# Last projection of a two-block transformer kernel: 12 of its 44 2x2 units by seven block products in place of eight

## The chip, the cores and the metric

The kernel runs on one core of one Trainium2 chip, in one launch. The metric is the time of one execution in device microseconds. Before the change it is 2310.49 us, the median of three runs (2310.07 to 2310.59).

## The reference, cut to what matters

The reference is two transformer blocks for 272 and then 256 tokens of 2048 features, in float32. The change touches the last matrix product of the second block and the norm and the residual sum behind it:

```
def conv_ffn(h, w_up, conv_w, w_down):
    ...
    gate, val = jnp.split(c, 2, axis=-1)
    return (jax.nn.silu(gate) * val) @ w_down          # (256, 5632) @ (5632, 2048)

def rms_norm(x, g):
    xf = x.astype(jnp.float32)
    y = xf * lax.rsqrt(jnp.mean(xf * xf, axis=-1, keepdims=True) + RMS_EPS)
    return (y * g.astype(jnp.float32)).astype(x.dtype)
...
    x = x + rms_norm(conv_ffn(h, ffn_w_up[i], ffn_conv[i], ffn_w_down[i]), norm_g[i, 3])
```

## The kernel before

Every large product is done in the type float32r with operands split in two: a high half (the value copied into float32r) and a low half (the value less its high half). A product of two blocks is three matmuls: high by high, high by low and low by high.

Weights come as chunks of 256 rows by 512 columns (512 KB): `raw[:, slot]` holds a chunk as two blocks of 128 rows, `kk` 0 and 1. A ring of four slots (`RING`) carries all 744 chunks of the kernel. Per chunk, four engines work in this order. SyncE's queue loads it (`raw`) when the low half of the chunk four earlier is done (`low_ready`). ScalarE copies it to the high half `wh` (function `high`, L584) when it has landed and TensorE has used the chunk four earlier (`chunk_used`). VectorE writes the low half `wl` (function `low`, L1046) when the high half is there. TensorE uses it when the low half is there. Each engine takes its instructions strictly in the order of its own program, so an instruction that waits holds up all behind it.

The last projection is `down2`: 88 chunks, four groups `g` of 512 output columns, 22 chunks `c` each. The activations stay put: `acth` and `actl` hold high and low halves of 44 blocks of 128 features by 256 tokens. TensorE goes through the groups one after the other, and for each chunk through its two row blocks and the two halves of the tokens `t` (L2571 to L2573): twelve matmuls of 128x128 by 128x512 per chunk. Output (`g`, `t`) has its own PSUM bank, `2 * g + t`. In the last group the last four chunks go through `t` = 0 first (`half_done`) and then `t` = 1, so that the first half of the tokens is done earlier.

When a group is through, ScalarE squares its two banks with a sum along the row (`square_rows`, L1010) and VectorE multiplies them by the gain into `ft` (`gain_rows`, L1801). Behind the last group the sum of squares becomes the scale of the row (`spread`: root on ScalarE, reciprocal on VectorE), and VectorE writes scale times `ft` plus the residual `ht` in pieces of 1024 or 512 columns (L1825), which SyncE stores. `ht` is the residual stream turned from feature rows to token rows by 32 transposes of VectorE (`block_of_h`, L1832), one after each of 16 low halves in the second and in the third group. GpSimd has nothing to do in this projection.

Of the kernel before, what the change touches and what calls it, by code (L numbers as in the profile page):

```python
# [21 lines left out]
F32 = mybir.dt.float32  # L22
F32R = mybir.dt.float32r
# [3 lines left out]
P = 128  # L27
# [83 lines left out]

N_PAIRS = 16
# [36 lines left out]
def program(nc, d):  # L149
    with ExitStack() as ctx:  # L150
# [21 lines left out]
        vec = persistent("vec", [P, N_VEC])  # L172
        ident = persistent("ident", [P, P])
# [100 lines left out]
        spent = at("spent", [P, 512], F32, LENT)  # L274

# [47 lines left out]
        ft_ready, out_ready = sem("ft_ready"), sem("out_ready")  # L323

# [186 lines left out]
        def _(pool):  # L511
# [11 lines left out]
            for s, (name, n) in enumerate(SUMS):  # L523
# [31 lines left out]
                for c, m in enumerate(CHUNK_LENGTHS):  # L555
# [13 lines left out]
                    pool.wait_ge(bk_ready, 2 * c + 2)  # L569


        @block.scalar
        def _(act):
# [433 lines left out]
            def square_rows(g, t):  # L1007
                if g + t:
                    act.wait_ge(squared, 2 * g + t)
                act.activation(spent[:], ps[:, 2 * g + t, :], ACT.Square, accum_out=squares[:, t, g:g + 1]).then_inc(squared, 1)  # L1010

            def squares_of_rows(g):
                if g < 3:
                    act.wait_ge(chunk_used, FIRST["down2"] + (g + 1) * CHUNKS["down2"])
                    square_rows(g, 0)
                    square_rows(g, 1)
                    if g == 2:
                        act.activation(warmed[:, 5:6], eps[:], ACT.Sqrt)
                    return
                act.wait_ge(partial_ready, 1)  # L1020
                for t in range(2):
                    if t == 0:
                        act.wait_ge(half_done, 1)
                    else:
                        act.wait_ge(chunk_used, N_CHUNKS)
                    square_rows(g, t)
                    act.wait_ge(squared, 7 + t)
                    act.activation(spread[:, t:t + 1], squares[:, t, 3:4], ACT.Sqrt, scale=1.0 / D,
                                   bias=partial[:, t:t + 1]).then_inc(spread_root, 1)

            plain("down2", squares_of_rows, ahead=8)


        @block.vector
        def _(dve):
# [762 lines left out]
            def gain_rows(g, t):  # L1798
                part = slice(512 * g, 512 * g + 512)
                dve.wait_ge(squared, 2 * g + t + 1)  # L1800
                dve.tensor_tensor(ft[:, t, part], ps[:, 2 * g + t, :], gain[:, part], ALU.mult).then_inc(ft_ready, 1)  # L1801

            def gained_rows(g):
                if g < 3:
                    group_full("down2", g)
                    if g == 0:
                        dve.wait_ge(gain_landed, 16)
                    gain_rows(g, 0)
                    gain_rows(g, 1)
                    if g == 2:  # L1810
                        dve.wait_ge(squared, 6)
                        dve.tensor_reduce(partial[:], squares[:, :, 0:3], mybir.AxisListType.X, ALU.add).then_inc(dve_step, 1)
                        dve.wait_ge(dve_step, steps.add())
                        dve.tensor_scalar(partial[:], partial[:], 1.0 / D, RMS_EPS, ALU.mult, ALU.add).then_inc(partial_ready, 1)
                    return
                dve.wait_ge(ht_ready, 32)
                for t in range(2):
                    gain_rows(g, t)
                    dve.wait_ge(spread_root, t + 1)
                    dve.reciprocal(spread[:, t:t + 1], spread[:, t:t + 1]).then_inc(spread_ready, 1)  # L1820
                    dve.wait_ge(spread_ready, t + 1)
                    dve.wait_ge(ft_ready, 7 + t)
                    for row, f0, f1 in OUT_PARTS:
                        if row == t:
                            dve.scalar_tensor_tensor(ft[:, t, f0:f1], ft[:, t, f0:f1], spread[:, t:t + 1], ht[:, t, f0:f1],  # L1825
                                                     ALU.mult, ALU.add).then_inc(out_ready, 1)

# [7 lines left out]
            def rows_of_h(g):  # L1835
                first, per = FIRST["down2"], CHUNKS["down2"]
                start = first + g * per + RING
                lows(start, 1, start % RING)
                gained_rows(g - 1)
                if g == 1:  # L1840
                    dve.wait_ge(h_ready, 48)
                for x in range(1, per):
                    low(start + x, (start + x) % RING)
                    if 2 <= x < 18:
                        block_of_h(16 * (g - 1) + x - 2)

# [11 lines left out]
        def _(pe):  # L1858
# [827 lines left out]
```

## Time and profile before

| | us |
|---|---|
| median of three runs | 2310.49 |
| the profiled execution, from start to end | 2310.11 |
| its span in the profile | 2308.0 |
| TensorE busy | 2297.3 |
| VectorE busy | 1558.6 |
| ScalarE busy | 1071.4 |
| GpSimd busy | 111.7 |
| the last projection's matmuls, first start to last start | 245.17 |

In the profile PE is TensorE's matmul, PEld its weight load, DVE is VectorE, ACT is ScalarE, POOL is GpSimd, SP is SyncE. A row of a group has the line of the program, the engine, the operation, the tile that is written and those that are read, the shape, the count, and behind the bar the busy time in all and the mean of one in ns, then the idle time of the engine just ahead of these instructions and what ended it. The granted clock of TensorE is 0.999 of full speed over the span. PE's busy time counts each matmul until it has drained, so consecutive matmuls overlap: their rate is read from the starts.

### The profile page before, as it was taken

Reading aid. Unit: us, or ns where it says so; the run is one execution under the profiler, and the core shown is the slowest. Engines: PE = TensorE matmul, PEld = TensorE weight load, DVE = VectorE, ACT = ScalarE, POOL = GpSimd, SP = SyncE. Lnnn points to the kernel's source line nnn. Section 1 sums busy time; section 2 is a strip of 40 time slices with the busy share of each in tenths; the row PEclk is TensorE's granted clock in tenths of the full one; section 3 lists DMA queues with packets and bytes.
Section 4 is the critical chain, followed back from the end, with each engine's and each line's share of the span. In section 5 each row is a group of like instructions: output and inputs, shape, how many; then the busy total and the mean of one; then the engine's idle time right before and its main releaser. Section 6 shows DMA issues by size and latency. Waiting matters only on the chain.

```text
span 2308.0 us, 49207 instructions
## 1 busy us (share of the span) xinstructions
PE 2297.3 (100%) x19330; PEld 2097.1 (91%) x19330; DVE 1558.6 (68%) x2008; ACT 1071.4 (46%) x1365; POOL 111.7 (5%) x144
## 2 busy tenths in 40 slices
PE   9999999999999999999999999999999999999998
PEld 9999999999999999998889999899888888888887
DVE  5688877748766666665444867559877777784664
ACT  6543444455444444444444556655444444444343
POOL 2000000012000000000000200012000000000000
PEclk9999999999999999999999999999999999999999
DMA  7554334355665665666556574465565665656664
GB/s 256 178 160 132 110 103 134 133 189 175 190 188 182 185 185 186 182 190 184 191 185 186 154 245 130 126 196 161 183 191 192 184 195 174 200 178 215 190 186 151
DMA packets 115688, 406.92 MB, mean 176 GB/s; under 512 B 12864, under 2 KB 17824, under 8 KB 115168
## 3 DMA queue, kind: packets, MB, share of 16 engines
q1 hardware_dynamic: 110672, 396.03, 55.1%
q10 hardware_dynamic: 4880, 8.87, 1.1%
q8 instruction: 111, 1.82, 0.3%
q14 instruction: 25, 0.20, 0.0%
HBM read 402.70 MB, written 2.15 MB: 175 GB/s over the span
## 4 chain that ended last, share of the span: by engine, by line
PE 98%; DVE 1%; ACT 0%; issue 0%; DVEq 0%; POOL 0%; ACTq 0%; POOLq 0%
PE ps L1919 26%; PE ps L1921 13%; PE ps L1924 8%; PE ps L1925 8%; PE ps L1926 8%; PE ps L2573 4%; PE ps L2571 4%; PE ps L2572 4%; PE ps L2131 3%; PE ps L2121 2%; PE ps L2123 2%; PE ps L2122 2%; PE ps L1884 2%; PE ps L1883 2%; PE ps L1882 2%; PE ps L2487 1%
## 5 line engine op out<-in xcount | busy, mean ns | idle before, releaser
L1046 DVE TENSOR_TENSOR wl<-raw,wh 128x1024 fp32r<-128x1024 f32 x742 | 906.9, 1234 | 623.8 <-ACT wh L584 622.2
L584 ACT ACTIVATE wh<-raw 128x1024 fp32r<-128x1024 f32 x742 | 776.6, 1057 | 898.6 <-PE ps L1921 370.1
L1919 PE MATMUL ps<-x,wh 128*128 128x512 f32 x1280 | 448.0, 393 | 0.0
L1924 PE MATMUL ps<-xx,wh 128*128 128x258 f32 (+3 forms) x1320 | 375.0, 284 | 0.0
L1925 PE MATMUL ps<-xx,wh 128*128 128x258 f32 (+3 forms) x1320 | 373.6, 283 | 0.0
L1926 PE MATMUL ps<-xx,wl 128*128 128x258 f32 (+3 forms) x1320 | 373.2, 283 | 0.0
L1921 PE MATMUL ps<-x,wl 128*128 128x256 f32 x1280 | 357.1, 279 | 0.0
L1919 PEld LDWEIGHTS ps<-x,wh 128*128 128x128 f32 x1280 | 239.8, 187 | 57.1
L1924 PEld LDWEIGHTS ps<-xx,wh 128*128 128x128 f32 x1320 | 248.2, 188 | 2.1 <-issue 0.8
L1925 PEld LDWEIGHTS ps<-xx,wh 128*128 128x128 f32 x1320 | 248.3, 188 | 0.4
L1926 PEld LDWEIGHTS ps<-xx,wl 128*128 128x128 f32 x1320 | 248.3, 188 | 0.0
L1921 PEld LDWEIGHTS ps<-x,wl 128*128 128x128 f32 x1280 | 239.8, 187 | 0.0
L1919 PE MATMUL ps<-xx,wh 128*128 128x512 f32 x640 | 225.0, 395 | 0.0
L1919 PE MATMUL ps<-act,wh 128*128 128x512 f32 x528 | 185.4, 393 | 0.0
L1921 PE MATMUL ps<-xx,wl 128*128 128x256 f32 x640 | 179.9, 281 | 0.0
L1921 PE MATMUL ps<-act,wl 128*128 128x256 f32 x528 | 149.3, 283 | 0.0
L1919 PEld LDWEIGHTS ps<-xx,wh 128*128 128x128 f32 x640 | 120.3, 188 | 27.9
L2573 PE MATMUL ps<-wh,act 128*128 128x512 f32 x352 | 138.9, 395 | 0.0
L2571 PE MATMUL ps<-wh,act 128*128 128x512 f32 x352 | 138.9, 395 | 0.0
L2572 PE MATMUL ps<-wl,act 128*128 128x512 f32 x352 | 138.9, 395 | 0.0
L1921 PEld LDWEIGHTS ps<-xx,wl 128*128 128x128 f32 x640 | 120.5, 188 | 0.0
L1919 PEld LDWEIGHTS ps<-act,wh 128*128 128x128 f32 x528 | 99.2, 188 | 22.9
(361 smaller groups left out, 3876.6 us busy)
## 6 DMA issues: line engine op xcount, KB each, us to landing
raw<-in_gate_up SPq DMA_DIRECT2D x176, 512.0 KB, 3.7
raw<-in_down SPq DMA_DIRECT2D x176, 512.0 KB, 4.2
raw<-in_up SPq DMA_DIRECT2D x176, 512.0 KB, 3.7
raw<-in_w_in SPq DMA_DIRECT2D x103, 512.0 KB, 3.8
raw<-in_in SPq DMA_DIRECT2D x48, 512.0 KB, 4.2
raw<-in_w_out SPq DMA_DIRECT2D x32, 512.0 KB, 4.4
raw<-in_out SPq DMA_DIRECT2D x32, 512.0 KB, 3.7
bias<-bias_rows ACTq DMA_DIRECT2D x1, 4096.0 KB, 25.9
```

The source lines that it names most:

```text
L584: act.activation(wh[:, slot], raw[:, slot], ACT.Copy).then_inc(high_ready, 1)
L1046: dve.tensor_tensor(wl[:, slot], raw[:, slot], wh[:, slot].bitcast(F32), ALU.subtract).then_inc(low_ready, 1)
L1882: pe.matmul(out, w_high, hi, start=(k == 0), stop=False)
L1919: pe.matmul(ps[:, 4 * parity + m, :].rearrange("p (s n) -> p s n", s=2), w_high, hi, start=(k == 0), stop=False)
L1921: last = pe.matmul(out, w_low, hi[:, 0], start=False, stop=(k == 2 * per - 1))
L1924: pe.matmul(out, w_high, high, start=(k == 0), stop=False)
L1925: pe.matmul(out, w_high, low, start=False, stop=False)
L1926: last = pe.matmul(out, w_low, high, start=False, stop=(k == 2 * per - 1))
L2131: last = pe.matmul(ps[o:o + rows, b, C * f:C * f + n], lhs[HEAD_ROWS[e]], rhs[HEAD_ROWS[e]], start=start, stop=stop)
L2571: pe.matmul(out, acth[:, k, tokens], wh[:, slot, kk, :], start=(k == 0), stop=False)
L2572: pe.matmul(out, acth[:, k, tokens], wl[:, slot, kk, :], start=False, stop=False)
L2573: last = pe.matmul(out, actl[:, k, tokens], wh[:, slot, kk, :], start=False, stop=(k == 2 * per - 1))
```

## The change

The output columns are now taken in two halves `p` of two column blocks `x` each, and the chunks are reordered on the host so that the chunks of a row pair `c` for both column blocks follow each other. Two such chunks are a unit: two row blocks by two column blocks of weights, against two token halves by two row blocks of activations, eight block products. 32 of the 44 units are done that way. In 12 (`SEVEN`) the 2x2 product is done by seven products (Winograd's form of Strassen's scheme), with sums of blocks on both sides: four mixed blocks of activations, four mixed blocks of weights. Four of the seven products are gathered in the four PSUM banks of the other half; behind the last seven-unit of a half, ScalarE copies the first of them to `ft` and VectorE adds up the corrections there (`combine`), and when the half is through adds each bank to its corner (`add_corner`).

GpSimd makes the four mixed activation blocks (from the sum of high and low halves) and, after ScalarE's high half, their low half. VectorE makes the mixed weights `mixes` from `raw`, ScalarE their high halves and VectorE their low halves. Only three of the four weight blocks of a seven-unit need halves of their own. The transposes now come two per eight-unit in the first half and one in the second. The squares are taken from `ft` and not from PSUM. The last two row pairs of the second half are done corner by corner.

The core of the diff:

```
+SEVEN = [(7, 10, 13, 16, 19), (3, 6, 8, 11, 13, 16, 18)]
+CORNERS = [(0, 0), (1, 0), (0, 1), (1, 1)]
...
 # GpSimd
+            for p in range(2):
+                for c in SEVEN[p]:
+                    q = SEVENTH[p][c]
+                    if q:
+                        pool.wait_ge(act_mix_ready, q)
...
+                    step(pool.tensor_tensor(whole_act[:], acth[:, 2 * c:2 * c + 2, :].bitcast(F32),
+                                            actl[:, 2 * c:2 * c + 2, :].bitcast(F32), ALU.add))
...
+                    pool.tensor_tensor(act_mix[:, 3], a11, a21, ALU.subtract)
+                    step(pool.tensor_tensor(act_mix[:, 0], a21, a22, ALU.add))
+                    step(pool.tensor_tensor(act_mix[:, 1], act_mix[:, 0], a11, ALU.subtract))
+                    pool.tensor_tensor(act_mix[:, 2], a12, act_mix[:, 1], ALU.subtract).then_inc(act_mixed, 1)
+                    pool.wait_ge(act_mixed, q + 1)
+                    pool.wait_ge(act_mix_split, q + 1)
+                    pool.tensor_tensor(act_mix_low[:], act_mix, act_mix_high[:].bitcast(F32),
+                                       ALU.subtract).then_inc(act_mix_ready, 1)
 # ScalarE
+            def seven_highs(p, c):
...
+                high(n, slot)
+                act.wait_ge(landed[slot + 1], 16 * ((n + 1) // RING + 1))
+                act.wait_ge(chunk_used, n + 1 - (RING - 1))
+                act.activation(wh[:, slot + 1, 1], raw[:, slot + 1, 1], ACT.Copy).then_inc(high_ready, 1)
+                act.wait_ge(act_mixed, q + 1)
+                if q:
+                    act.wait_ge(mix_used, q)
+                act.activation(act_mix_high[:], act_mix, ACT.Copy).then_inc(act_mix_split, 1)
+                for x in range(2):
+                    act.wait_ge(mixed, 2 * q + x + 1)
+                    act.activation(mix_high[x][:], mixes[x], ACT.Copy).then_inc(mix_split, 1)
 # VectorE
+            def mix_weights(p, c):
...
+                dve.wait_ge(landed[slot], 16 * (n // RING + 1))
+                dve.wait_ge(landed[slot + 1], 16 * (n // RING + 1))
+                if q:
+                    dve.wait_ge(mix_split, 2 * q)
+                    dve.wait_ge(mix_ready, 2 * q)
+                dve.tensor_tensor(mixes[0], raw[:, slot + 1], raw[:, slot:slot + 2, 0], ALU.subtract).then_inc(mixed, 1)
+                dve.wait_ge(mixed, 2 * q + 1)
+                step(dve.tensor_tensor(mixes[1][:, 0], raw[:, slot + 1, 1], mixes[0][:, 0], ALU.subtract))
+                dve.tensor_tensor(mixes[1][:, 1], raw[:, slot, 1], mixes[1][:, 0], ALU.subtract).then_inc(mixed, 1)
...
+            def seven_lows(p, c):
...
+                mix_weights(p, c)
+                low(n, slot)
...
+                dve.tensor_tensor(wl[:, slot + 1, 1], raw[:, slot + 1, 1], wh[:, slot + 1, 1].bitcast(F32),
+                                  ALU.subtract).then_inc(low_ready, 1)
+                for x in range(2):
+                    dve.wait_ge(mix_split, 2 * q + x + 1)
+                    dve.tensor_tensor(mix_low[x][:], mixes[x], mix_high[x][:].bitcast(F32), ALU.subtract).then_inc(mix_ready, 1)
...
+            def combine(p):
...
+                dve.wait_ge(first_kept, p + 1)
...
+                step(dve.tensor_tensor(corner(p, 1, 0), ps[:, bank + 2, :], corner(p, 0, 0), ALU.add))
+                step(dve.tensor_tensor(corner(p, 0, 1), ps[:, bank + 3, :], corner(p, 1, 0), ALU.add))
+                dve.tensor_tensor(corner(p, 1, 1), ps[:, bank + 1, :], corner(p, 0, 1), ALU.add)
+                dve.tensor_tensor(corner(p, 1, 0), ps[:, bank + 1, :], corner(p, 1, 0), ALU.add).then_inc(combined, 1)
 # TensorE
+                pe.wait_ge(low_ready, n + 1)
+                product(extra[0], act_of(k, 0), weight_of(slot, 0), start, stop)
+                product(sums[0], act_of(k + 1, 0), weight_of(slot, 1), False, False).then_inc(chunk_used, 1)
+                pe.wait_ge(low_ready, n + 2)
+                pe.wait_ge(act_mix_ready, q + 1)
+                product(sums[2], mixed_act(2), weight_of(slot + 1, 1), False, False).then_inc(chunk_used, 1)
+                pe.wait_ge(mix_ready, 2 * q + 1)
+                product(extra[1], mixed_act(0), mixed_weight(0, 0), start, stop)
+                product(extra[3], mixed_act(3), mixed_weight(0, 1), start, stop)
+                pe.wait_ge(mix_ready, 2 * q + 2)
+                product(extra[2], mixed_act(1), mixed_weight(1, 0), start, stop)
+                product(sums[1], act_of(k + 1, 1), mixed_weight(1, 1), False, False).then_inc(mix_used, 1)
```

`product` is the three matmuls. Where the instructions stand now, at three places. First VectorE in the middle of the projection; before, around the seam of the second and third group (`wl<-raw,wh` is a low half, `ht<-lead` a transpose, `ft<-ps,gain` a gain):

```order
L1046 TENSOR_TENSOR wl<-raw,wh 128x1024
L1832 STREAM_TRANSPOSE ht<-lead 32x16x32
L1046 TENSOR_TENSOR wl<-raw,wh 128x1024 x5
L1801 TENSOR_TENSOR ft<-ps,gain 128x512 x2
L1046 TENSOR_TENSOR wl<-raw,wh 128x1024 x2
```

After, from the first seven-unit (unit 7 of the first half) to the start of the second (`ft<-raw` and `ft<-raw,ft` are the mixed weights, `mix_low<-ft,mix_high` their low halves):

```order
L1892 TENSOR_TENSOR ft<-raw 128x1024
L1894 TENSOR_TENSOR ft<-raw,ft 128x512
L1895 TENSOR_TENSOR ft<-raw,ft 128x512
L1121 TENSOR_TENSOR wl<-raw,wh 128x1024
L1904 TENSOR_TENSOR wl<-raw,wh 128x512
L1908 TENSOR_TENSOR mix_low<-ft,mix_high 128x1024 x2
L1121 TENSOR_TENSOR wl<-raw,wh 128x1024 x2
L1877 STREAM_TRANSPOSE ht<-lead 32x16x32 x2
```

A seven-unit puts three mixing passes ahead of its low halves and two low halves of mixed weights behind them; the transposes stand in pairs behind the eight-units. Second GpSimd, which had no instruction here, has these for each seven-unit (`vec` holds the mixed activations; shapes are partitions by elements):

```order
L608 TENSOR_TENSOR whole_act<-act 128x512
L612 TENSOR_TENSOR vec<-whole_act 128x128
L613 TENSOR_TENSOR vec<-whole_act 128x128
L614 TENSOR_TENSOR vec<-vec,whole_act 128x128
L615 TENSOR_TENSOR vec<-whole_act,vec 128x128
L618 TENSOR_TENSOR act_mix_low<-vec,act_mix_high 128x512
```

The first five of the next unit follow directly on the sixth of this one. Third VectorE at the end of the projection (`sums` is the scale of a row). Before:

```order
L1801 TENSOR_TENSOR ft<-ps,gain 128x512
L1820 RECIPROCAL sums<-sums 128x1
L1825 SCALAR_TENSOR_TENSOR ft<-ft,sums,ht 128x1024 x2
L1801 TENSOR_TENSOR ft<-ps,gain 128x512
L1820 RECIPROCAL sums<-sums 128x1
L1825 SCALAR_TENSOR_TENSOR ft<-ft,sums,ht 128x1024
L1825 SCALAR_TENSOR_TENSOR ft<-ft,sums,ht 128x512 x2
```

After (`ft<-ps,ft` is the add of a bank to its corner):

```order
L1951 RECIPROCAL sums<-sums 128x1
L1946 SCALAR_TENSOR_TENSOR ft<-ft,sums,ht 128x1024
L1929 TENSOR_TENSOR ft<-ps,ft 128x512
L1946 SCALAR_TENSOR_TENSOR ft<-ft,sums,ht 128x1024
L1937 TENSOR_TENSOR ft<-ft,gain 128x512
L1941 TENSOR_REDUCE sums<-squares 128x1
L1942 TENSOR_SCALAR sums<-sums 128x1
L1929 TENSOR_TENSOR ft<-ps,ft 128x512
L1937 TENSOR_TENSOR ft<-ft,gain 128x512
L1951 RECIPROCAL sums<-sums 128x1
L1946 SCALAR_TENSOR_TENSOR ft<-ft,sums,ht 128x1024
L1946 SCALAR_TENSOR_TENSOR ft<-ft,sums,ht 128x512 x2
```

The add of the last corner now stands behind the second row pass of the first token half, a gain and two small sums.

## Rows read from the trace of the kernel before

**Rows 1.** The page: busy time by engine, the chain's shares by engine, and one costly group.

```profile
PE 2297.3 (100%) x19330; PEld 2097.1 (91%) x19330; DVE 1558.6 (68%) x2008; ACT 1071.4 (46%) x1365; POOL 111.7 (5%) x144
...
PE 98%; DVE 1%; ACT 0%; issue 0%; DVEq 0%; POOL 0%; ACTq 0%; POOLq 0%
...
L1046 DVE TENSOR_TENSOR wl<-raw,wh 128x1024 fp32r<-128x1024 f32 x742 | 906.9, 1234 | 623.8 <-ACT wh L584 622.2
```

**Rows 2.** Groups by line, 2050 us on: operation, shapes, count, busy us, mean ns, idle.

```profile
L2573 PE MATMUL ps<-wh,act 128*128 128x512 f32 x352 | 138.9, 395 | 0.0
...
L1046 DVE TENSOR_TENSOR wl<-raw,wh 128x1024 fp32r<-128x1024 f32 x89 | 108.8, 1225 | 99.4 <-ACT wh L584 99.4
L584 ACT ACTIVATE wh<-raw 128x1024 fp32r<-128x1024 f32 x88 | 93.1, 1060 | 137.8 <-PE ps L2573 134.6 <-PE ps L1921 3.2
...
L1832 DVE STREAM_TRANSPOSE ht<-lead 32x512 f32<-32x512 f32 x32 | 22.5, 702 | 0.9
...
L1801 DVE TENSOR_TENSOR ft<-ps,gain 128x512 f32<-128x512 f32 x8 | 5.2, 684 | 6.2 <-ACT spent L1010 6.2
L1825 DVE SCALAR_TENSOR_TENSOR ft<-ft,sums,ht 128x1024 f32<-128x1024 f32 (+1 forms) x5 | 5.1, 1068 | 0.1
L1010 ACT ACTIVATE spent<-ps 128x512 f32<-128x512 f32 x8 | 4.7, 593 | 9.1 <-PE ps L2573 9.0
```

**Rows 3.** Timeline, TensorE, first and last matmul of the last projection: start us, duration us.

```profile
2055.17 0.39 PE L2571 MATMUL ps<-wh,act 128*128 128x512 f32 x1
...
2300.34 0.40 PE L2573 MATMUL ps<-wh,act 128*128 128x512 f32 x1
```

**Rows 4.** Chain that ended last, from the last matmul on: start us, us, what.

```profile
2300.77 0.70 ACT spent L1010 x2
...
2301.49 0.69 DVE ft L1801
...
2302.29 1.28 DVE ft L1825
2303.57 0.66 DVEq L150
2304.23 0.66 DVE ft L1825
```

**Rows 5.** Waits, 2080 to 2300 us: who waited for whom, us in total, times, longest.

```profile
DVE wl L1046 <- ACT wh L584: 93.3, 77, 1.9
```

**Rows 6.** Groups by form, GpSimd, whole run.

```profile
L565 POOL TENSOR_TENSOR bk<-b,pinv 128x128 f32<-128x128 f32 x1 | 0.5, 467 | 0.1
```

**Rows 7.** Groups by form, VectorE, whole run: a split of half a chunk.

```profile
L1041 DVE TENSOR_TENSOR wl<-raw,wh 128x512 fp32r<-128x512 f32 x4 | 2.8, 691 | 0.4 <-ACT wh L647 0.4
```

**Rows 8.** Timeline, VectorE (three rows), then GpSimd (two), 217.5 to 220.5 us.

```profile
217.69 0.69 DVE L1245 TENSOR_TENSOR fac<-kn,pe 128x512 f32<-128x512 f32 x1
218.29 1.77 DVE L1246 TENSOR_TENSOR fac<-z,pe 128x512 f32<-128x512 f32 x1
219.99 1.68 DVE L1374 TENSOR_TENSOR am<-ga,lmask 128x512 f32<-128x512 f32 x1
...
217.73 1.79 POOL L565 TENSOR_TENSOR bk<-b,pinv 128x512 f32<-128x512 f32 x1 [48.61 <-DVE b L1233]
219.60 1.52 POOL L567 TENSOR_TENSOR bk<-z,pinv 128x512 f32<-128x512 f32 x1
```

**Rows 9.** Timeline, VectorE (two rows), then GpSimd (two), 311 to 314.5 us.

```profile
311.26 1.76 DVE L1046 TENSOR_TENSOR wl<-raw,wh 128x1024 fp32r<-128x1024 f32 x1 [1.48 <-ACT wh L584]
313.58 0.69 DVE L1468 TENSOR_TENSOR tn<-tn,ps 128x512 f32<-128x512 f32 x1 [0.57 <-PE ps L2131]
...
310.65 1.29 POOL L565 TENSOR_TENSOR bk<-b,pinv 128x512 f32<-128x512 f32 x1 [49.95 <-PE ps L2131]
312.02 2.05 POOL L567 TENSOR_TENSOR bk<-z,pinv 128x512 f32<-128x512 f32 x1
```

**Rows 10.** DMA issues, 2095 to 2255 us: count, KB each, median us from issue to landing.

```profile
raw<-in_down SPq DMA_DIRECT2D x57, 512.0 KB, 4.3
```

More of the change, by code:

```diff
@@ L109 @@
     _n += _k
+SEVEN = [(7, 10, 13, 16, 19), (3, 6, 8, 11, 13, 16, 18)]
+SEVENTH = [{c: q + sum(map(len, SEVEN[:p])) for q, c in enumerate(rows)} for p, rows in enumerate(SEVEN)]
+SEVENS = [len(SEVEN[0]), len(SEVEN[0]) + len(SEVEN[1])]
+CORNERS = [(0, 0), (1, 0), (0, 1), (1, 1)]
 N_PAIRS = 16
@@ L1796, in _ @@
             feed_forward("up2", True)
[L1798 to L1826, printed above, removed]
             def block_of_h(x):
@@ new lines, in add_corner @@
+            def add_corner(p, e):
+                x, t = CORNERS[e]
+                dve.wait_ge(combined, p + 1)
+                if p and t == 0:
+                    dve.wait_ge(half_done, x + 1)
+                elif p and x == 0:
+                    dve.wait_ge(chunk_used, N_CHUNKS - 2)
+                else:
+                    dve.wait_ge(chunk_used, FIRST["down2"] + 44 * (p + 1))
+                dve.tensor_tensor(corner(p, x, t), ps[:, 4 * p + 2 * x + t, :], corner(p, x, t), ALU.add).then_inc(corner_ready, 1)
@@ new lines, in finish_rows, with spread_of_rows @@
+            def finish_rows(t, x0, x1):
+                for row, f0, f1 in OUT_PARTS[x0:x1]:
+                    dve.scalar_tensor_tensor(ft[:, t, f0:f1], ft[:, t, f0:f1], spread[:, t:t + 1], ht[:, t, f0:f1],
+                                             ALU.mult, ALU.add).then_inc(out_ready, 1)
+            def spread_of_rows(t):
+                dve.wait_ge(spread_root, t + 1)
+                dve.reciprocal(spread[:, t:t + 1], spread[:, t:t + 1]).then_inc(spread_ready, 1)
+                dve.wait_ge(spread_ready, t + 1)
@@ new lines, in _ @@
+            dve.wait_ge(chunk_used, FIRST["down2"])
+            dve.wait_ge(h_ready, 48)
+            blocks = 0
+            for p in range(2):
+                for c in range(6 * (1 - p), 22):
+                    if c in SEVEN[p]:
+                        seven_lows(p, c)
+                    else:
+                        lows(row_chunk(p, c), 2, row_chunk(p, c) % RING)
+                        if p and c in (1, 2):
+                            gain_corner(0, 2 * c - 2)
+                            gain_corner(0, 2 * c - 1)
+                        ahead = min(32, blocks + (1 if p and c < 20 else 2))
+                        for x in range(blocks, ahead):
+                            block_of_h(x)
+                        blocks = ahead
+                    if c == SEVEN[p][-1] + 2:
+                        combine(p)
+                    if p and c == 0:
+                        for e in range(4):
+                            add_corner(0, e)
@@ L2575, in _ @@
                         last.then_inc(chunk_used, 1)
[L2576 to L2577 removed]
+                if t == 0:
+                    last.then_inc(half_done, 1)
 def _features(v):
```

219 lines of the change are left out of this document (155 added, 64 removed).

## The prediction

> **What bounds the kernel now.** I read the page first. Its busy times have TensorE at 2297.3 of 2308.0 us and the chain of waits gives it 98% [rows 1]; the reader sees an engine that is never waited out, so only fewer matmuls, or a new wait of TensorE, can move the time. Then the groups of instructions from 2050 us to the end, which is the last projection: three matmul lines with 352 matmuls each (one of them in [rows 2]) and, beside them, the split of the weights, L584 on ScalarE and L1046 on VectorE. Then the first and the last matmul of that projection in the order of time [rows 3]: 2300.34 - 2055.17 = 245.17 us for 1055 steps, 0.2324 us a matmul. The 395 ns of [rows 2] is one matmul from start to drained; the step is what counts. VectorE's waits there, 93.3 us for ScalarE [rows 5], are slack that the change may use. Last the chain behind the last matmul [rows 4].
>
> I call a unit two row blocks by two column blocks: two loaded chunks, eight products of three matmuls, 24 x 0.2324 = 5.58 us. A seven-unit is 21 x 0.2324 = 4.88 us.
>
> **What is removed.** 12 units lose three matmuls: 36 x 0.2324 = 8.37 us, all on the path. Nothing else leaves it: the chunks that are loaded, 88, and the matmul's shape stay.
>
> **VectorE in a seven-unit.** Durations: 1.23 us for 128x1024 and 0.70 for a transpose [rows 2], 0.69 for 128x512 [rows 7]. Queued behind each other, the next starts 0.09 early (0.69 at 217.69, next at 218.29 [rows 8]), so 1.14 and 0.60. Before, a unit asks for two splits, 2.28. A seven-unit asks for four passes of 1024 columns (first mixed block, whole low half, two mixed low halves) and three of 512: 4 x 1.14 + 3 x 0.60 = 6.36, and 0.12 for each of two waits on its own result: 6.6 us, against 4.88 on TensorE. An eight-unit asks for 2.28 and, with the transposes spread over the units, 0.70 (second half) or 1.40 (first). At the closest spacing, seven then eight, that is 6.6 + 2.98 = 9.6 against 4.88 + 5.58 = 10.46. Alone, VectorE would hold the pace and the extra waits of TensorE inside the unit would be met. ScalarE needs 3 x 1.06 + 2 x 0.6 = 4.4 us in a seven-unit [rows 2] and is not the limit either.
>
> **GpSimd beside it.** GpSimd gets two passes of 128x512 (1.29 us each, the first of its rows in [rows 9]) and four of 128x128 (0.47 [rows 6]) per seven-unit. [Rows 8] shows what such a pass does to VectorE. L1245 takes 0.69; the next, L1246, equally large, takes 1.77 while a GpSimd pass reads; then GpSimd's pass is the one that is long; then VectorE's L1374 takes 1.68. They take turns, whole instruction by whole instruction, and VectorE loses 1.0 to 1.1 us to a pass of 1.2 to 1.3, the pass less some 0.2. In [rows 9] a split of 1.23 takes 1.76 in the same way, but L1468, with one input in PSUM, takes 0.69 in the middle of a GpSimd pass. So the price is 2 x 1.04 + 4 x 0.25 = 3.1 us of VectorE per seven-unit, wherever VectorE has passes with two SBUF inputs queued; transposes, and sums with PSUM, are free of it. The 0.25 is an estimate, 0.47 less 0.2.
>
> The Trainium skill, SBUF — State Buffer, section "Who interferes with whom", has this as a rule: a VectorE instruction with two SBUF inputs and a GpSimd instruction that reads SBUF hold one shared read path in turn, each for its whole length. The traces here agree (0.69 against 1.77 us). One could also argue from averages: over the whole run the split averages 1234 ns, in the last projection, where GpSimd is idle, 1225 [rows 1, 2], 9 ns apart. By that the price would be nothing and the sum would be rival A's; by the turns it is 3.1 us. I take the turns: the average holds few splits that met GpSimd.
>
> **Does it fit then?** Seven then eight in the second half: 6.6 + 3.1 + 2.98 = 12.7 against 10.46, 2.2 us short. This spacing stands at units 6, 11 and 16 of the second half (the seven-units are 3, 6, 8, 11, 13, 16, 18): 6.6 us. Seven, eight, eight there: 15.7 against 16.04, 0.4 to spare, three times after the first, 1.2. In the first half (7, 10, 13, 16, 19) seven, eight, eight: 6.6 + 3.1 + 2 x 3.68 = 17.1 against 16.04, but of that 2.8 is transposes, beside which GpSimd can run: 0 to 1.0 short each. A lead could pay for this: a chunk's high half may be made when TensorE has used the chunk four earlier, and by the walk above (high, then low, behind two mixing passes) the low half of a seven-unit is done some 3.5 us before TensorE asks. That pays for the first half, 0 to 5 short. It doesn't pay in the second, because the lead goes round a ring: a chunk is loaded only when the low half four chunks earlier is done, takes 4.3 us to land [rows 10], and the mixing waits for both landed chunks of the unit. 4.3 + 2.6 for the mixes + 2.1 for the two long GpSimd passes + 1.7 for the low halves is 10.7 per two units, against 10.46. So 6.6 - 1.2 = 5.4 in the second half and about nothing in the first; with a rest of lead I take 5.0 us of TensorE waits. The ends are 0 (GpSimd's passes fall into gaps and beside transposes) and 9.6 (6.6 with no recovery, and 3 of the first half).
>
> **The seam between the halves.** TensorE's wait for the combined sums is met if VectorE gets to them in time. Their four passes (0.68 each, one input in PSUM, 2.7 us) stand behind the splits of the first half's last unit, whose inputs are there while TensorE does unit 20, with over a unit left: nothing, or a microsecond or two if VectorE comes late; that is in the range. The gains and sums of the four corners (8 x 0.68 = 5.4 us) fall among five units without sevens, with 5 x (5.58 - 2.98) = 13 us to spare.
>
> **The tail.** Now the last matmul (ends 2300.57 as a step) is followed by the square at 2300.77, the gain, the reciprocal and three row passes ending 2304.89, and then the store [rows 4]: 4.3 us plus the store. After, an add of 0.68 comes ahead of the square, and VectorE is not free. With E the end of matmuls and 2.79 us for each of the four last corners, the second corner's sum is there at E - 5.4. VectorE's queue from there: add to -4.7, wait for the square (0.70) to -3.9, gain to -3.1, reciprocal and a row pass of 1.28 to -1.7, third add to -1.1, the other row pass to +0.1, gain to +0.8, the two small sums to +1.0, and only then the last add, to +1.7. The square starts at +1.75 in place of +0.2: 1.6 us later, 0.7 for the add and 0.8 of queue. From there the chain is the old one.
>
> **Sum.** -8.4 + 5.0 + 1.6 = -1.8 us. The profiled execution took 2310.11 us (span 2308.0 and 2.1 around it), 0.4 under the median of 2310.49. 2310.1 - 1.8 = 2308.3 us. A measurement can tell 0.2%, 4.6 us, from no change; so this is no change.
>
> **Rival A: GpSimd costs VectorE nothing.** -8.4 + 1.6 = -6.8: 2303.3 us, 0.29% faster. For it: VectorE waits 93.3 us in this stretch, there are free slots for 12 x 4.4 us of GpSimd. Against it: the sums and low halves of the activations follow directly on ScalarE's split of the same unit, when VectorE has its longest queue. It holds if the waits stay under 2.2 us. 0.30.
>
> **Rival B: VectorE becomes the bound in every stretch.** If each long GpSimd pass costs VectorE 1.7 us, as L565 and L567 took when they were themselves held up (1.79, 2.05 [rows 8, 9]), the price is 4.4 us a seven-unit, 1.3 more. The pairs are then 3.5 short, 10.5; the triples of the second half 0.9, 2.7; those of the first up to 2.3, 5 to 9, less 3.5 of lead: 15 to 18 us of waits, and -8.4 + 1.6 + 16.5 = +9.7: 2319.8 us, slower. It decides from 11.4 us of waits on (8.4 - 1.6 + 4.6). Against it: in [rows 8] GpSimd's long time is a wait during which VectorE works. 0.10.
>
> **Rival C: ScalarE or the DMA ring, not GpSimd.** The mixing pass needs both chunks landed, where the split needed one. If landing is late by 1 us where two loads are issued close together, the pairs lose 3 us without GpSimd: -3.8, 2306.3 us. It lies within the forecast's range and I count it there.
>
> **Chances and range.** Forecast, waits of 2.2 to 11.4 us, within 0.2%: 0.60. Faster by over 0.2%: 0.30 (A). Slower: 0.10 (B). The range reaches to no waits at all, 2303.2, and up to 9.6 us of waits, 2312.9; above that lies B.
>
> **What would show it.** Right: in the profile after, the matmul groups of the last projection count 1020; TensorE has short waits for VectorE's low halves, each under 3 us, gathered at the low halves of the chunks around units 6 to 8, 11 to 13 and 16 to 18 of the second half; the split beside GpSimd goes from 1.23 to 1.5 and more; the square after the last matmul starts some 1.8 us after it. Wrong: no waits of TensorE between 2090 and 2290 us, VectorE's passes at 1.23 beside GpSimd's (A); waits in every unit from the first seven on (B); TensorE waiting for landed chunks with VectorE idle (C).

## The result, and the profile after

The changed kernel takes 2316.57 us (2315.55 to 2318.01, 8 runs), before 2310.54 beside it: ratio 1.0026, interval 1.0015 to 1.0037. The forecast was 2308.3; the measured time is 3.7 us above the range's upper end. The profiled execution took 2315.82 us, span 2313.5.

The page of the changed kernel, first the busy times by engine, then the chain's shares by engine, answers to [rows 1]:

```profile
PE 2294.2 (99%) x19294; PEld 2088.2 (90%) x19294; DVE 1651.9 (71%) x2086; ACT 1098.1 (47%) x1403; POOL 204.5 (9%) x216
...
PE 90%; DVE 7%; issue 1%; DMA 1%; ACT 0%; DVEq 0%; SPq 0%; POOL 0%; ACTq 0%; POOLq 0%
```

TensorE's share of the chain fell from 98 to 90%, VectorE's rose from 1 to 7%. So the end now hangs on VectorE in some stretches; the average of 99% busy for TensorE does not show that. TensorE's timeline in the last projection (start us, duration us, in brackets the idle time before and who ended it) answers to [rows 3]:

```profile
2055.26 0.39 PE L2701 MATMUL ps<-wh,act 128*128 128x512 f32 x1
...
2128.04 0.50 PE L2701 MATMUL ps<-wh,act 128*128 128x512 f32 x1 [1.10 <-DVE wl L1121]
...
2223.88 0.40 PE L2703 MATMUL ps<-wh,act 128*128 128x512 f32 x1
2226.50 0.50 PE L2701 MATMUL ps<-wh,act 128*128 128x512 f32 x1 [2.22 <-DVE wl L1121]
...
2227.43 0.63 PE L2701 MATMUL ps<-wh,act 128*128 128x512 f32 x1
2227.85 0.63 PE L2702 MATMUL ps<-wl,act 128*128 128x512 f32 x1
...
2304.45 0.40 PE L2703 MATMUL ps<-wh,act 128*128 128x512 f32 x1
```

2304.45 - 2055.26 = 249.19 us for 1019 steps of 0.2324, which are 236.82: TensorE waits 12.4 us where 5.0 was forecast. The second row is a unit of the first half that starts 1.3 us late. The fourth is the longest wait: 2226.50 less 2223.88 less a step is 2.39. Behind it the matmuls start 0.42 us apart, not 0.23. The same stretch by windows (us, then busy time and count for five engines, granted clock, DMA share, GB/s):

```profile
core 0: us, PE busy (x) PEld busy (x) DVE busy (x) ACT busy (x) POOL busy (x), PEclk, DMA share, GB/s
...
2224.00:2227.00 3.00, 0.78 (x4) 0.45 (x3) 2.97 (x4) 1.91 (x2) 2.84 (x4) 1.00 0.00 1
2227.00:2230.40 3.40, 3.40 (x10) 2.60 (x9) 3.40 (x4) 1.20 (x3) 0.63 (x1) 0.52 0.69 227
```

The granted clock is 1.00 up to the wait's end and 0.52 in the 3.4 us behind it, nearly all of them at the lower of the two levels, 1.2 GHz. That costs 1.6 us (3.4 x 0.48).

VectorE's groups from 2050 us to the end (busy us, mean ns of one, idle before) answer to [rows 2]:

```profile
L1121 DVE TENSOR_TENSOR wl<-raw,wh 128x1024 fp32r<-128x1024 f32 x77 | 100.0, 1327 | 10.3 <-ACT wh L634 10.0
L1908 DVE TENSOR_TENSOR mix_low<-ft,mix_high 128x1024 fp32r<-128x1024 f32 x24 | 35.4, 1516 | 0.0
L1877 DVE STREAM_TRANSPOSE ht<-lead 32x512 f32<-32x512 f32 x32 | 22.5, 702 | 0.9
L1895 DVE TENSOR_TENSOR ft<-raw,ft 128x512 f32<-128x512 f32 x12 | 16.3, 1359 | 0.4
...
L1904 DVE TENSOR_TENSOR wl<-raw,wh 128x512 fp32r<-128x512 f32 x12 | 12.7, 1062 | 0.0
```

The split went from 1225 to 1327 ns, the low halves of the mixed weights take 1516 for the same 128x1024, and the 128x512 passes 1062 to 1359 where [rows 7] has 691. Transposes stay at 702. The six groups without the transposes are busy for 195.3 us.

The timeline of VectorE through one triple (seven-unit 10 of the first half and the eight-units 11 and 12), then of GpSimd:

```profile
2104.41 1.23 DVE L1892 TENSOR_TENSOR ft<-raw 128x1024 f32<-128x1024 f32 x1
2105.67 0.69 DVE L1894 TENSOR_TENSOR ft<-raw,ft 128x512 f32<-128x512 f32 x1
2106.40 1.74 DVE L1895 TENSOR_TENSOR ft<-raw,ft 128x512 f32<-128x512 f32 x1
2108.06 2.32 DVE L1121 TENSOR_TENSOR wl<-raw,wh 128x1024 fp32r<-128x1024 f32 x1
2110.30 0.94 DVE L1904 TENSOR_TENSOR wl<-raw,wh 128x512 fp32r<-128x512 f32 x1
2111.17 2.88 DVE L1908 TENSOR_TENSOR mix_low<-ft,mix_high 128x1024 fp32r<-128x1024 f32 x2
2113.97 2.62 DVE L1121 TENSOR_TENSOR wl<-raw,wh 128x1024 fp32r<-128x1024 f32 x2
2116.62 1.44 DVE L1877 STREAM_TRANSPOSE ht<-lead 32x512 f32<-32x512 f32 x2
2118.09 2.36 DVE L1121 TENSOR_TENSOR wl<-raw,wh 128x1024 fp32r<-128x1024 f32 x2
2120.48 1.44 DVE L1877 STREAM_TRANSPOSE ht<-lead 32x512 f32<-32x512 f32 x2
...
2106.29 1.30 POOL L618 TENSOR_TENSOR act_mix_low<-vec,act_mix_high 128x512 fp32r<-128x512 f32 x1 [6.91 <-ACT act_mix_high L1067]
2107.67 1.63 POOL L608 TENSOR_TENSOR whole_act<-act 128x512 f32<-128x512 f32 x1
```

VectorE has no gap: from the first row to the next mixing pass at 2121.95 it is 17.5 us, against 16.04 on TensorE. GpSimd's passes lie beside the mixing and the low halves, none of those shown beside a transpose (of the 67 from 2085 us on it is 3). The waits from 2080 to 2300 us (who for whom, us in all, times, longest) say why, and answer to [rows 5]:

```profile
POOL act_mix_low L618 <- ACT act_mix_high L1067: 109.5, 12, 26.5
ACT wh L634 <- DMA raw<-in_down: 40.3, 24, 3.4
...
PE ps L2701 <- DVE wl L1121: 6.7, 6, 2.2
```

GpSimd is early by 7.5 us a unit (109.5 less the 26.5 at the seam, over eleven) and stands until ScalarE has the high half of the same unit; then all its passes follow in one run, when VectorE has most to do. ScalarE's 40.3 us of waits for loads speak for rival C; e10 to e12 try it. The tail, all engines, answers to [rows 4]:

```profile
2305.52 0.69 DVE L1929 TENSOR_TENSOR ft<-ps,ft 128x512 f32<-128x512 f32 x1
...
2306.25 0.63 ACT L1088 ACTIVATE spent<-ft 128x512 f32<-128x512 f32 x1 [1.94 <-DVE ft L1929]
...
2307.01 0.69 DVE L1937 TENSOR_TENSOR ft<-ft,gain 128x512 f32<-128x512 f32 x1 [0.79 <-ACT spent L1088]
```

The last square starts 2306.25 - 2304.68 = 1.57 us after the last step. From the last step to the span's end it is 8.8 us, before 7.4: 1.4 more, forecast 1.6.

-8.4 + 12.4 + 1.4 = +5.4, on 2310.1: 2315.5 us, measured 2315.8. All terms but the waits came about as forecast.

### The profile page after: what moved, and what is told of

Read it like the earlier page. It is cut to its first block, busy times and chain, and to the rows that moved or that the text cites. A ratio compares the mean times of both kernels' runs of the same rounds, so it can differ in the third digit from the quotient of the medians.

```text
span 2313.5 us, 49282 instructions
## 1 busy us (share of the span) xinstructions
PE 2294.2 (99%) x19294; PEld 2088.2 (90%) x19294; DVE 1651.9 (71%) x2086; ACT 1098.1 (47%) x1403; POOL 204.5 (9%) x216
## 4 chain that ended last, share of the span: by engine, by line
PE 90%; DVE 7%; issue 1%; DMA 1%; ACT 0%; DVEq 0%; SPq 0%; POOL 0%; ACTq 0%; POOLq 0%
PE ps L2058 26%; PE ps L2060 13%; PE ps L2063 8%; PE ps L2064 8%; PE ps L2065 8%; PE ps L2270 3%; PE ps L2260 2%; PE ps L2261 2%; PE ps L2262 2%; DVE wl L1121 2%; PE ps L2023 2%; PE ps L2022 2%; PE ps L2021 2%; DMA raw<-in_down 1%; DVE mix_low L1908 1%
## 5 line engine op out<-in xcount | busy, mean ns | idle before, releaser
L1121 DVE TENSOR_TENSOR wl<-raw,wh 128x1024 fp32r<-128x1024 f32 x730 | 897.9, 1245 | 533.8 <-ACT wh L634 531.7
L634 ACT ACTIVATE wh<-raw 128x1024 fp32r<-128x1024 f32 x730 | 763.9, 1058 | 837.7 <-PE ps L2060 369.6
L2701 PE MATMUL ps<-wh,act 128*128 128x512 f32 x280 | 111.7, 399 | 6.9 <-DVE wl L1121 6.7
L552 POOL TENSOR_TENSOR sq_sum<-sq_sum,sq 128x256 f32<-128x256 f32 (+2 forms) x99 | 88.3, 892 | 327.4 <-ACT sq L649 318.6
L2260 PE MATMUL ps<-xx,wh 128*128 128x260 f32 x384 | 114.7, 299 | 0.3 <-issue 0.3
```

The source lines that it names most:

```text
L552: pool.tensor_tensor(sq_sum[:, 0:n], sq_sum[:, 0:n], sq[:, slot, 0:n], ALU.add).then_inc(sq_added, 1)
L634: act.activation(wh[:, slot], raw[:, slot], ACT.Copy).then_inc(high_ready, 1)
L1121: dve.tensor_tensor(wl[:, slot], raw[:, slot], wh[:, slot].bitcast(F32), ALU.subtract).then_inc(low_ready, 1)
L2260: pe.matmul(out, w_high, hi, start=(k == 0), stop=False)
L2701: pe.matmul(out, left_high, right_high, start=start, stop=False)
```

## The experiments

All timed beside the kernel before (2310.2 to 2310.4 us in these series). T1: GpSimd's turns make VectorE late. T2: VectorE's own added passes do. T3: the loads do. "Waits" is the time from the first to the last matmul of the last projection less 0.2324 us a step. "VectorE" is the busy time of its six groups without transposes.

| run | us | ratio to before, interval | waits | VectorE |
|---|---|---|---|---|
| changed | 2316.57 | 1.0026 (1.0015 to 1.0037) | 12.4 | 195.3 |
| e1_small_sums | 2303.27 | 0.9970 (0.9958 to 0.9982) | -0.2 | 163.3 |
| e2_two_sevens | 2310.03 | 0.9998 (0.9989 to 1.0007) | -0.1 | |
| e3_spacing_three | 2313.40 | 1.0014 (1.0005 to 1.0023) | 8.8 | |
| e4_timed | 2305.80 | 0.9981 (0.9972 to 0.9990) | 2.3 | 179.7 |
| e5_timed_spaced_tail | 2304.82 | 0.9974 (0.9964 to 0.9984) | 0.3 | |
| e6_sums_later | 2306.40 | 0.9983 (0.9974 to 0.9992) | 2.8 | 182.9 |
| e7_high_earlier | 2306.67 | 0.9984 (0.9975 to 0.9993) | 3.1 | 184.7 |
| e8_twice | 2327.27 | 1.0074 (1.0060 to 1.0088) | 23.7 | 207.2 |
| e9_transposes_second | 2322.55 | 1.0053 (1.0040 to 1.0067) | 18.2 | 192.7 |
| e10_small_transposes | 2311.91 | 1.0008 (0.9999 to 1.0017) | 8.5 | 196.1 |
| e11_small_transposes_half_loads | 2305.54 | 0.9978 (0.9969 to 0.9988) | 1.5 | 191.7 |
| e12_half_loads | 2312.91 | 1.0011 (1.0002 to 1.0020) | 9.8 | 195.2 |

**e1_small_sums**

```diff
-step(pool.tensor_tensor(whole_act[:], acth[:, 2*c:2*c+2, :] ...
+few = 4 if q else P
+step(pool.tensor_tensor(whole_act[:, :, 0:2*few], acth[:, 2*c:2*c+2, 0:2*few] ...
 (the other five passes likewise)
```

> Edit: from the second seven-unit on, GpSimd's six passes read and write 4 columns where they had 128 (8 where they had 256), so the mixed activations of 11 units are left out; every instruction, wait and semaphore stays. Theory T1 (GpSimd's passes take turns with VectorE's and so make the low halves late): TensorE's 12.4 us of waits in the last projection fall to about 2 (the short pauses at semaphores stay), so -8.4 + 2 + 1.5 of tail: 2305 to 2306.5 us, VectorE's split back at about 1.23 us. Theory T2 (VectorE's own added passes are too much even alone): waits stay above 8 us, 2312 us or more. Theory T3 (the chunks land too late for the mixing pass): the same 2312 or more, with VectorE idle before the mixing passes.

2303.27 us, 1.7 under T1's range, and no wait of TensorE for VectorE is left. VectorE's groups:

```profile
L1909 DVE TENSOR_TENSOR mix_low<-ft,mix_high 128x1024 fp32r<-128x1024 f32 x24 | 28.4, 1221 | 3.4 <-ACT mix_high L1071 3.3
...
L1893 DVE TENSOR_TENSOR ft<-raw 128x1024 f32<-128x1024 f32 x12 | 14.7, 1225 | 2.9 <-issue 2.6
...
L1896 DVE TENSOR_TENSOR ft<-raw,ft 128x512 f32<-128x512 f32 x12 | 8.3, 692 | 0.4
```

The same three passes take 1221, 1225 and 692 ns once GpSimd reads next to nothing. T2 and T3 in their plain form fall: VectorE's own work fits, and so do the loads. This is rival A's number (2303.3), had GpSimd cost nothing. The turns cost 195.3 - 163.3 = 32 us of VectorE, 2.9 for each of the 11 units that were changed. The Trainium skill, SBUF — State Buffer, "Who interferes with whom", says that a VectorE instruction with two SBUF inputs contends with a GpSimd instruction that reads SBUF; the traces agree, 1516 against 1221 ns.

**e2_two_sevens**

```diff
-SEVEN = [(7, 10, 13, 16, 19), (3, 6, 8, 11, 13, 16, 18)]
+SEVEN = [(7,), (3,)]
```

> Edit: one unit in each half by seven products (7 and 3), the rest of the change stays. It measures what does not grow with the number of units: the seam between the halves and the tail. -1.4 for six matmuls, +1.5 of tail. All theories that put the loss into the seven-units (T1, T2, T3): waits of under 1 us, 2310.3 to 2311.5 us. If the seam or the spread transposes cost by themselves (theory T4): 2313 us or more.

2310.03 us, 0.3 under the range, no waits, tail 8.8 us as in the changed kernel. Seam and spread transposes cost nothing by themselves, with one seven-unit a half; T4 falls.

**e3_spacing_three**

```diff
-SEVEN = [..., (3, 6, 8, 11, 13, 16, 18)]
+SEVEN = [..., (3, 6, 9, 12, 15, 18)]
```

> Edit: the second half's units are 3, 6, 9, 12, 15, 18 in place of 3, 6, 8, 11, 13, 16, 18: one fewer, none two apart; the first half as it is. T1 and T2 (VectorE's work per unit against its distance): the waits of 2.4, 0.9 and 0.2 us at the close units go and with the first the stretch at half the granted clock (1.7 us); small waits of 0.2 to 0.4 us stay: +0.7 for the unit lost, -4 to -5 of waits, 2312 to 2313.5 us. T3 (loads): the loads are as close in the triples, half of it stays, 2315 us.

2313.40 us, as T1 and T2 expect. The clock stays up, but the triples still wait: 1.0 to 1.3 us at three units of the first half, 1.2 at unit 3 of the second and 0.2 to 0.6 at four behind it.

**e4_timed, e6_sums_later, e7_high_earlier**

```diff
 # e6 and e4: GpSimd, ahead of its sums
 pool.wait_ge(act_mix_ready, q)
+pool.wait_ge(low_ready, row_chunk(p, c) - 2)
 # e7 and e4: ScalarE, from the seven-unit to the end of the unit ahead of it
+if c + 1 in SEVEN[p]:
+    q = SEVENTH[p][c + 1]
+    act.wait_ge(act_mixed, q + 1)
+    ...
+    act.activation(act_mix_high[:], act_mix, ACT.Copy).then_inc(act_mix_split, 1)
```

> Edit: GpSimd's first five passes for a seven-unit wait until VectorE has split the first unit behind the seven-unit before (so they start beside its transposes), and ScalarE makes the high half of the mixed activations one unit earlier, so that GpSimd's last pass too falls ahead of the unit, beside the transposes. All units, all work stay. T1: what VectorE loses to the passes falls by about half in the triples, the five waits of about 1 us in the first half mostly go, the close units of the second half stay: 2311 to 2313.5 us, and the low halves of the mixed weights (1516 ns) back to 1.25 to 1.35 us. T2 and T3: no change, 2315 to 2318 us.

> Edit: of the two moves of e4_timed only the first, GpSimd's sums wait for the split of the first unit behind the seven-unit before; the high half of the mixed activations stays where it was. T1 (turns of GpSimd and VectorE): the five sums are two thirds of what VectorE pays (1.04 + 4 x 0.25 of 3.0 us), so half to three quarters of the 10.8 us that e4_timed gave: 2308 to 2311 us. Rival T5 (it was not VectorE but TensorE's own wait for the mixed activations' low half): no change, 2315 to 2318 us.

> Edit: of the two moves of e4_timed only the second, ScalarE makes the high half of the mixed activations one unit earlier and GpSimd's last pass follows it; the sums for the next seven-unit follow directly as before. T1: the one long pass moved to the transposes, a third of the price, but the sums now fall on the mixing passes: 2311 to 2315 us. T5: the whole gain of e4_timed, 2305 to 2307 us.

2305.80, 2306.40 and 2306.67 us: all three are under T1's ranges, by 5.2, 1.6 and 4.3 us. No instruction is gone, only the time at which GpSimd starts is other. VectorE, then GpSimd, in e6:

```profile
2112.99 1.44 DVE L1878 STREAM_TRANSPOSE ht<-lead 32x512 f32<-32x512 f32 x2
...
2113.10 1.30 POOL L609 TENSOR_TENSOR whole_act<-act 128x512 f32<-128x512 f32 x1 [5.24 <-DVE wl L1122]
```

The sum of 128x512 takes 1.30 us beside the two transposes, which keep their 0.72 each. In e6 30 of GpSimd's 67 passes from 2085 us on stand beside a transpose, in the changed kernel 3. T5 expected e7's time (2305 to 2307), but falls by e6, which leaves ScalarE's high half where it was and was to change nothing. T1's proportion fell too: each move alone was to bring at most three quarters of the gain of both, and each brought over nine tenths. With each move over half of the 32 us stays with VectorE (182.9 and 184.7 against 163.3), and TensorE waits for only 3: what VectorE pays is not passed on one for one.

**e8_twice**

```diff
-step(pool.tensor_tensor(whole_act[:], ...
+for again in range(2): step(pool.tensor_tensor(whole_act[:], ...
```

> Edit: the changed kernel with GpSimd's first long pass (128x512) done twice in each seven-unit, same data. T1: VectorE pays another 1.0 to 1.1 us in each of 11 units, and as there is no lead left TensorE waits that much longer: +11 to +13, and +1.7 for each wait that grows past 2 us and lets the granted clock fall: 2328 to 2334 us. T5 or a VectorE that is late by its own work: GpSimd waits 8 to 10 us for ScalarE in each unit, so a pass more costs nothing: 2316 to 2318 us.

2327.27 us, 10.7 more, 0.7 under the range. One of VectorE's groups:

```profile
L1908 DVE TENSOR_TENSOR mix_low<-ft,mix_high 128x1024 fp32r<-128x1024 f32 x24 | 40.7, 1735 | 0.0
```

One pass more in GpSimd's 7.5 us of standing idle costs VectorE 11.9 us and TensorE 11.3. That the two are so near is in part luck: the granted clock falls four times here and once in the changed kernel, some 1.6 us each, so 4.8 of the 11.3 are clock and the waits themselves grew by 6.5, where 11 to 13 were expected. Over the runs that move or repeat GpSimd's passes alone (e1, e4, e6, e7, changed, e8) there is a knee: from 163 to 185 us of VectorE the waits grow by 3, from 185 to 207 by 21, of which the falling clock is 6.

**e9_transposes_second, e10_small_transposes**

```diff
 # e9
-ahead = min(32, blocks + (1 if p and c < 20 else 2))
+ahead = min(32, blocks + (3 if p else 0))
 # e10
-dve.transpose(rows[:, :, 32*q:32*q+32], h[32*q:32*q+32, :, ...
+dve.transpose(rows[:, 0:1, 32*q:32*q+32], h[32*q:32*q+32, 0:1, ...
```

> Edit: the 32 transposes leave the first half; in the second half each eight-unit takes three until they are done (it took one). No work is left out, GpSimd as in the changed kernel. T1 in its sharper form (each stretch has a budget of VectorE time, what is over it becomes TensorE's wait one for one): first half without waits, -4.6 us; in the second half 11 eight-units carry 1.4 us more each, 10 to 13 us of waits more and one or two falls of the granted clock of 1.7: 2322 to 2328 us. Rival T6 (only passes of GpSimd that meet the first low half of a seven-unit count, by the delay they give it; VectorE's other work is hidden): first half as before, the time within 2 us of 2316.6.

> Edit: each of the 32 transposes turns one block of 32x32 where it turned sixteen, and the last row passes add the projection itself where they added the transposed rows, so most of the transposed residual is left out; GpSimd's passes as in the changed kernel. T1, budget form: VectorE gets 2.6 us back per triple of the first half (it was 1.5 over) and 0.65 per eight-unit of the second, GpSimd's turns stay (splits and mixing still at 1.3 to 1.5 us): 1 to 3 us of waits left, 2305.5 to 2308 us. T6: the turns stay, so the waits stay: 2314 to 2317 us.

2322.55 us, in the range of the budget form, but by two misses that cancel: three short waits of 0.2 to 0.6 us stayed in the first half, where the waits fell by 2.6 us and not 4.6, and the second half's grew by 8.4 (with one fall of the clock in both runs), where 10 to 13 were expected. And 2311.91 us, which neither theory expected: with 4 x (702 - 202 ns) = 2.0 us a triple given back (the expectation said 2.6; it was 1.5 over), the first half still waits 0.4 to 0.6 us three times. T6 falls by both. VectorE's timeline in e10, the triple of above:

```profile
2113.20 2.89 DVE L1121 TENSOR_TENSOR wl<-raw,wh 128x1024 fp32r<-128x1024 f32 x2
2116.12 0.44 DVE L1877 STREAM_TRANSPOSE ht<-lead 32x32 f32<-32x32 f32 x2
2116.59 2.36 DVE L1121 TENSOR_TENSOR wl<-raw,wh 128x1024 fp32r<-128x1024 f32 x2
2118.98 0.44 DVE L1877 STREAM_TRANSPOSE ht<-lead 32x32 f32<-32x32 f32 x2
2120.82 1.23 DVE L1892 TENSOR_TENSOR ft<-raw 128x1024 f32<-128x1024 f32 x1 [1.40 <-issue]
```

The loads there, 2095 to 2255 us (count, KB, median us from issue to landing):

```profile
raw<-in_down SPq DMA_DIRECT2D x56, 512.0 KB, 4.4
```

And the one load that is issued between 2116 and 2117.5 us:

```profile
L524 SPq DMA_DIRECT2D raw<-in_down x1: 332/332/332, 2116.3 to 2116.3; - x1
...
DMA to landing us min/median/max: 4.5/4.5/4.5
```

Now VectorE stands idle for 1.40 us before the mixing pass at 2120.82; the row names no releaser ("issue"). But the second low half of the first row ends at 2116.1, the load of the freed slot is issued at 2116.3 and lands 4.5 us later, at 2120.7, and the mixing pass, which needs both chunks of its unit, starts then. So behind VectorE's budget there seems to stand a second bound, a loop: low half, load, landing, mixing, low half. The turns stretch it as well: without them, in e1, TensorE never waits, with the same loads.

**e11_small_transposes_half_loads, e12_half_loads**

```diff
+if name == "down2":
+    sp.dma_start(raw[:, j, 0], weights[i*RING + j, :, 0]).then_inc(landed[j], 16)
```

> Edit: e10_small_transposes, and each load of the last projection brings only the first of the chunk's two row blocks (256 KB in place of 512; the second keeps older values). e10_small_transposes fell short of the budget form of T1: TensorE still waits 0.5 us a triple in the first half while VectorE stands idle 1.4 us before the mixing passes, for a chunk that lands 4.6 us after the low half four chunks earlier. Theory T7 (behind VectorE's budget stands a second bound, the loop low half, load, landing, mixing, low half, which the turns stretch too): with loads that land 1 to 2 us sooner the first half's three waits go and the 1.7 us waits of the close units fall to about 0.5: 2306.5 to 2309 us. If the loop is not the cause (VectorE's turns alone): no change, 2311 to 2313 us.

> Edit: the changed kernel with only the half loads of e11_small_transposes_half_loads (the second row block of each chunk keeps older values). T7 with both bounds: in the first half VectorE has 17.5 us of work for 16.04 and its budget is the nearer bound, so the waits of about 1 us stay there; in the second the close units gain and the fall of the granted clock goes: 2311 to 2314 us. If the loop alone decides: 2306 to 2309 us. If it plays no part here: 2316 to 2317 us.

2305.54 us (under the range) and 2312.91. The loads of e11:

```profile
raw<-in_down SPq DMA_DIRECT2D x60, 256.0 KB, 2.6
```

With loads of 2.6 us, the first half of e11 has no wait left and the low halves of its seven-units from 10 on are 5.1 us ahead of TensorE, with most of VectorE's turns still there (191.7 us, in e10 196.1). So in e10 the loop was the bound of the first half. In e12, where the transposes are back, unit 13 of the first half starts like this (TensorE's timeline):

```profile
2128.02 0.50 PE L2704 MATMUL ps<-wh,act 128*128 128x512 f32 x1 [1.07 <-DVE wl L1124]
```

1.2 us late, and the two behind it 1.0, as in the changed kernel: there the budget is the nearer bound and shorter loads (2.7 us) change nothing. The 2.5 us that e12 gained (12.4 to 9.8) are all in the second half, and 1.6 of them are the fall of the clock that did not come. The two close units that waited longest still wait 1.86 and 1.59 us (units 8 and 13; in the changed kernel 2.39 and 0.87). So T7's loop decides in e10, where VectorE has time to spare; in the changed kernel it is worth little but for the clock, and VectorE's budget is most of it there.

**e5_timed_spaced_tail**

```diff
 (e3's and e4's edits, and in the tail)
 add_corner(1, 2)
-finish_rows(0, 1, 2)
 gain_corner(1, 2)
 partial_of(1)
 add_corner(1, 3)
+finish_rows(0, 1, 2)
 gain_corner(1, 3)
```

> Edit: three together. GpSimd's passes timed beside the transposes (as in e4_timed), the second half's units 3, 6, 9, 12, 15, 18 (as in e3_spacing_three), and in the tail the second row pass of the first row block put behind the last corner's sum. T1: -7.7 for 33 matmuls, 0.5 of waits (the one at unit 3, 0.4, stays), tail +0.7 to +1.1 in place of +1.5: 2303.5 to 2304.5 us, the fastest of the correct kernels. If the three do not add up (theory T4: what is left is in the seam and does not move): 2305 us or more.

2304.82 us, the fastest run with the whole computation, 0.26% (0.16 to 0.36) faster than before, though 0.3 above the expected range. The waits are 0.3 us. The edit of the tail brought nothing (timeline, all engines):

```profile
2293.92 0.40 PE L2706 MATMUL ps<-wh,act 128*128 128x512 f32 x1
...
2295.29 1.27 DVE L1949 SCALAR_TENSOR_TENSOR ft<-ft,sums,ht 128x1024 f32<-128x1024 f32 x1
...
2295.40 0.63 ACT L1091 ACTIVATE spent<-ft 128x512 f32<-128x512 f32 x1 [1.63 <-DVE ft L1932]
...
2296.48 0.68 DVE L1940 TENSOR_TENSOR ft<-ft,gain 128x512 f32<-128x512 f32 x1
```

The last square starts earlier, 1.25 us after the last step, but the moved row pass now stands ahead of the gain, which starts 2.33 us after the last step, as it did in the changed kernel (2307.01 - 2304.68).

## Why the prediction was wrong

Right: the 8.4 us of matmuls; that VectorE alone holds the pace at 6.6 us a seven-unit (e1); the turns as the mechanism, and about their price, 3.1 forecast, 2.9 measured; the tail, 1.6 and 1.4; and which waits are TensorE's, those for low halves.

The step that failed is "Does it fit then?", its result "I take 5.0 us of TensorE waits". By units, 12.4 is:

- First half: forecast "about nothing", measured 3.4 at units 10, 13, 16 and 19. Two sentences carried that. "Of that 2.8 is transposes, beside which GpSimd can run": it can (e6), but it did not, because its last pass waited for ScalarE's high half of the same unit and its sums stood right behind that pass. I took a cover to be used because it was there, without asking what releases the covered work. And "That pays for the first half": the lead was 3.4 us at unit 7, as worked out (3.5), and 0.1 at unit 10, so it paid for one triple of four. The rows below are VectorE's at unit 7, those of unit 10 stand above (2104.41 and 2108.06). From mixing pass to mixing pass it is 17.3 us, 1.3 over TensorE's 16.04. And the low half ends 6.0 us after the mixing pass starts, at unit 7 3.8, because at unit 10 GpSimd's passes begin ahead of it (2106.29), at unit 7 behind its start (2090.28). The ring of loads had no part in this: in e12, with shorter loads, the lead at unit 10 is 0.1 as well; in e1, without GpSimd's reads, it is 3.9.

```profile
2087.10 1.23 DVE L1892 TENSOR_TENSOR ft<-raw 128x1024 f32<-128x1024 f32 x1
...
2089.69 1.22 DVE L1121 TENSOR_TENSOR wl<-raw,wh 128x1024 fp32r<-128x1024 f32 x1
```

- Seam: forecast "13 us to spare" over five units, measured 1.2 at unit 3 of the second half. VectorE's sums of the corners wait for TensorE's last matmul of the first half, for 2.53 us in e6 (below), where the first half has a lead. So a lead is cut there (4.2 us at unit 0, 1.7 at unit 1), and three units, 16.7 us of TensorE, have to cover the sums, the gains, two eight-units and the mixing of unit 3. In the changed kernel that takes VectorE 17.1 us, from 2179.68 to 2196.77, and it starts late, for want of a lead. In e4 and e6 unit 3 still waits 0.4 and 1.1.

```profile
2174.59 2.48 DVE L1930 TENSOR_TENSOR ft<-ps,ft 128x512 f32<-128x512 f32 x4 [2.53 <-PE ps L2704]
```

- Second half: forecast 5.4, measured 3.9 at units 6, 8, 13, 16 and 18. VectorE's 12.7 us for seven and eight came out, 12.9 and 12.7 from mixing pass to mixing pass at units 6 and 11, 12.0 at 16; with shorter loads (e12) 13.0, 12.7 and 11.9, so it was this sum that held and not the loop of 10.7. But the waits behind them, 2.4, 0.9 and 0.2, are not three times 2.2: unit 11 was 3.7 us ahead again, in part because TensorE took 17.7 us from unit 8 to unit 11 in place of 16.0, the lower clock's 1.6 among them.
- Not forecast: 1.6 us for the fall of the granted clock, and the rest, 2.3 us, in pauses of about 0.1, at the matmul behind each wait and at the mixed weights' low halves, which come just in time once VectorE is late.

The outcome is near rival B's (VectorE the bound, though unit 7 of the first half and unit 11 of the second do not wait), at a lower price than rival B needed. I had put its threshold into the price of a pass (4.4 us a unit); it lay in where the passes fall.

## What to carry to other kernels

Work on GpSimd that shares VectorE's reads is neither free nor dear by itself: it costs little while VectorE's period has time to spare (e6, e7), and over half of it becomes TensorE's wait where the period is full (e8). So add up the period of every spacing with the turns in it, and look at what releases GpSimd's passes before counting cover; one semaphore wait moved many of them under the transposes and was worth 10 us. A lead is no store for many periods: here one period used it up, and at the seam an instruction that waits for the consumer ended it.

## What was not expected of the hardware

After waits of 2.28 to 3.17 us the granted clock fell to the lower level in some cases and not in others: in the changed kernel after 2.39; in e8 after 2.28, 2.32, 2.60 and 3.17, not after 2.54; in e9 after the first wait of 2.37, not after the others of 2.37 and 2.39, nor after 3.00. Two windows of e9 (columns as above), behind the wait of 3.00 and behind the first of 2.37:

```profile
2196.30:2200.00 3.70, 3.70 (x16) 3.03 (x17) 3.70 (x4) 1.52 (x3) 0.15 (x1) 1.00 0.64 235
2214.80:2218.70 3.90, 3.90 (x10) 3.08 (x11) 3.90 (x4) 1.56 (x3) 0.98 (x2) 0.56 0.69 213
```

The granted clock is 1.00 in the one and 0.56 in the other. No wait of 1.86 us or less was followed by a fall, and none lay between 1.86 and 2.28. What decides there was not tried and stays open.

Half the bytes brought the load from 4.4 us to 2.6 (e10 and e11), so the last 256 KB cost 1.8 us in this stretch. In e10, where the load is in a loop with the compute, that was worth 6.4 us (2311.91 to 2305.54); in the changed kernel 3.7 (e12).
